# Stick-breaking attention in a hybrid layer: the mask moved into the score's accumulation, and the suffix product made from two float32r products

## The chip, the core and the metric

The kernel runs on one core of one Trainium2 chip. The metric is the device time in microseconds (us). Three runs of the kernel before took 3732.57, 3734.17 and 3734.45 us, so the median is 3734.17 us.

## The reference, cut to what matters

One decoder layer: input projection, stick-breaking attention (8 heads of 64), an S5 state-space part, an output mix and a gated convolutional FFN. It handles a prompt of 2048 tokens, and 8 sample tokens that each attend to 8192 cached keys. The part that changes is this:

```python
z = q @ k.T * HEAD_DIM**-0.5 + bias
mask = k_pos[None, :] < q_pos[:, None]
log_keep = jnp.where(mask, log_sigmoid(-z), 0.0)       # = -softplus(z)
later = cumsum(log_keep, reverse=True) - log_keep      # sum over the keys between s and t
w = jnp.where(mask, exp(log_sigmoid(z) + later), 0.0)
out = w @ v
```

Written with sp = softplus(z), the log of a weight is z minus the sum of sp over this key and all later ones.

## The kernel before, in words

`stage_attention` is one of several stages. Five engines each run a list of their own, with semaphores between them. A *unit* is one block of scores, transposed: 128 keys (index j) by up to 512 queries (chunk c of 4). Per head there are NU = 40 units, chunk 3 first (16 units), then chunk 2 (12), chunk 1 (8) and chunk 0 (4), and in a chunk the keys go from late to early. The first four units of a chunk lie on the diagonal and have 128, 256, 384 and 512 columns; all others are 512 wide. Of the 40 units, 21 are off the diagonal with j > 0.

Each engine runs a loop over steps s = 0..39 for each head, with the stages of a unit software-pipelined over the steps:

- PE at step s: the scores of unit s (`z`, L1415: two float32r products that carry rounded and rest parts and the bias) into one of NZ = 5 PSUM banks. Then for unit u = s - 3: `negtri` (a triangle of -1) times X[u] (L1425), on the diagonal also `ident` times `fillm` (L1428, adds -1e30 where masked), then `negones` times S[u-1] (L1433), and `logw_ready` goes up. Then, at odd u, weights times V for the last two units (L1448), and at even steps up to 32 four pages of the cached V of the sample sequence (L1382). `negtri`, `negones`, `ident` and V products are plain float32.
- ACT at step s: exp (L1197) and ln(1 + .) (L1199) of unit s into X (NX = 4 buffers), then exp of unit s - 3 into Wt (L1205). At some steps it also rounds parts of q and k of the next head (L1169 to L1175).
- DVE at step s: softplus of unit s - 1 from X and the bank (L1302, X in place). At steps 0 to 31 it then multiplies two cached K pages by the query (L1331) and sums over the head dimension (L1336). This is the attention of one sample sequence, which goes along with each head of the prompt.
- POOL (GpSimd) in `sums_round`: on the diagonal X times `keepm` in place (L1135) and into S (L1142); then S[u] = S[u-1] + X[u] (L1148). S has two buffers, so S[u] waits for `logw_ready` of unit u - 1:

```python
pool.wait_ge(logw_ready, b * NU + u)
...
pool.tensor_tensor(new[:, r:], old[:, r:], x[:, r:], ALU.add).then_inc(s_part, 1)
```

  PE reads S[u-1] with unit u, so S[u] is wanted only one unit later.
- SP queues all loads: K pages into a ring of 8 places, V pages into one of 16, and q, k, v of the next head.

Around steps 32 to 37 the sample sequence is finished: a softplus and scans over its 64 pages, `finish_sequence` (DVE L1261 makes `own`, PE L1390 sums it, DVE L1265 keeps it), PE L1456 and L1457, and `turn_queries`. Heads 1 to 6 are a hardware loop; heads 0 and 7 are written out.

Of the kernel before, what the change touches and what calls it, by code (L numbers as in the profile page):

```python
# [22 lines left out]
P = 128  # L23
# [3 lines left out]
NS = 8  # L27
# [877 lines left out]
def stage_attention(nc, A, keep):  # L905
# [16 lines left out]
    MASKS = [sum(diag(v) for v in range(u + 1)) for u in range(NU)]  # L922
    with ExitStack() as ctx:
# [9 lines left out]
        X = m.sb("X", [P, NX, CH])  # L933
        Wt = m.sb("Wt", [P, NW, CH])
        S = m.sb("S", [P, 2, CH])
        o_sb = m.sb("o_sb", [HD, 2, CH])
        o_odd = m.sb("o_odd", [HD, CH])
        bias_all, bias_left = m.sb("bias_all", [P, H]), m.sb("bias_left", [P, H])
        bias_part, bias_rows = m.sb("bias_part", [P, BP, H], F32R), m.sb("bias_rows", [P, H])
        bias_now = m.sb("bias_now", [P, 1])  # L940
        wide = m.sb("wide", [P, CH])
        negtri, negones = m.sb("negtri", [P, P]), m.sb("negones", [P, P])
        one = m.sb("one", [P, 1])
        keepm, fillm = m.sb("keepm", [P, P]), m.sb("fillm", [P, P])
        Kr = m.sb("Kr", [P, KSLOTS, PP, AW])
        Vr = m.sb("Vr", [P, VSLOTS, PP, AW])
        prod = m.sb("prod", [P, 2, PP * AW])
# [4 lines left out]
        table_in = x_s[0:1].bitcast(I32)  # L952
        R = m.sb("R", [P, H, NPG + 1])
        heads = m.sb("heads", [P, AW])
        own = m.sb("own", [P, AW])
# [12 lines left out]
        z_ready, e_ready, l_ready, sp_ready, sp_masked = (  # L968
            m.sem(n) for n in ("z_ready", "e_ready", "l_ready", "sp_ready", "sp_masked"))
# [14 lines left out]
        Q_AT = K_END + 5  # L984
# [28 lines left out]
        with nc.Block() as block:  # L1013
# [93 lines left out]
            def _(pool):  # L1107
                pool.memset(negtri[:], -1.0).then_inc(consts, 1)
                pool.memset(negones[:], -1.0).then_inc(consts, 1)
                pool.memset(keepm[:], 1.0).then_inc(consts, 1)  # L1110
# [4 lines left out]
                pool.wait_ge(consts, 6)  # L1115
                pool.memset(wide[:], 1.0).then_inc(wide_set, 1)
                pool.wait_ge(wide_set, 1)
                pool.memset(kh1[HD:P, :].bitcast(F32), 1.0).then_inc(wide_set, 1)
                pool.wait_ge(wide_set, 2)
# [4 lines left out]
                sel(out=keepm[:], in_=keepm[:], compare_op=ALU.is_gt, fill=0.0, base=0, pattern=[[1, P]],  # L1124
                    channel_multiplier=-1).then_inc(consts, 1)
                sel(out=fillm[:], in_=fillm[:], compare_op=ALU.is_gt, fill=MASKED, base=0, pattern=[[1, P]],
                    channel_multiplier=-1).then_inc(consts, 1)
                pool.wait_ge(consts, 9)

                def sums_round(b):  # L1130
                    for u in range(NU):
                        o, x = cols(u), X[:, u % NX, :]
                        if diag(u):
                            pool.wait_ge(sp_ready, b * NU + u + 1)
                            pool.tensor_tensor(x[:, o:o + P], x[:, o:o + P], keepm[:], ALU.mult).then_inc(sp_masked, 1)  # L1135
                        if U[u][1] == 0:
                            continue
                        old, new = S[:, (u - 1) % 2, :], S[:, u % 2, :]
                        pool.wait_ge(logw_ready, b * NU + u)
                        if diag(u):  # L1140
                            pool.wait_ge(sp_masked, b * MASKS[-1] + MASKS[u])
                            pool.tensor_tensor(new[:, o:o + P], x[:, o:o + P], keepm[:], ALU.mult).then_inc(s_part, 1)  # L1142
                        else:
                            pool.wait_ge(sp_ready, b * NU + u + 1)
                        if steps(u) == 2 or not diag(u):
                            r = o + P if diag(u) else 0
                            pool.wait_ge(s_part, b * SUMS[-1] + SUMS[u - 1])
                            pool.tensor_tensor(new[:, r:], old[:, r:], x[:, r:], ALU.add).then_inc(s_part, 1)  # L1148
# [5 lines left out]
            def _(act):  # L1154
# [3 lines left out]
                act.activation(bias_part[:, 0, :], bias_all[:], ACT.Copy).then_inc(bias_rounded, 1)  # L1158
                for n in range(1, BP):
                    act.wait_ge(bias_cut, n)  # L1160
                    act.activation(bias_part[:, n, :], bias_left[:], ACT.Copy).then_inc(bias_rounded, 1)

                def split(b, c):
# [8 lines left out]
                    if c == NCH - 1:  # L1172
                        act.wait_ge(wide_set, 2)
                        act.wait_ge(bias_now_ready, b + 1)
# [11 lines left out]
                def round_(b, steps, first, last, rest):  # L1186
                    for s in steps:
# [13 lines left out]
                        if u is not None:  # L1201
# [3 lines left out]
                            act.activation(Wt[:, u % NW, cols(u):], bank[:, u % NZ, cols(u):], ACT.Exp).then_inc(w_ready, 1)  # L1205
                        r, u = behind(b, s, LAG + 2, first, rest)
# [19 lines left out]
                        if s == K_END + 5:  # L1226
# [8 lines left out]
            def _(dve):  # L1235
# [4 lines left out]
                dve.wait_ge(consts, 9)  # L1240
# [49 lines left out]
                def round_(b, steps, first, last, rest):  # L1290
                    for s in steps:
# [17 lines left out]
                        if u is not None and U[u][1] == 0:  # L1309
# [5 lines left out]
                            if alone:  # L1315
                                dve.tensor_copy(o_sb[:, c % 2, 0:alone], o_odd[:, 0:alone]).then_inc(alone_copied, 1)
# [1188 lines left out]
```

## Time and profile before

| | us |
|---|---|
| median of three runs | 3734.17 |
| profiled execution, own time | 3731.39 |
| its span | 3729.7 |
| PE busy | 3346.6 (90%) |
| DVE busy | 2056.5 (55%) |
| ACT busy | 1408.0 (38%) |
| POOL busy | 759.2 (20%) |
| attention stage | about 738 to 1797 of the span |

Times below are from the start of the span. PE is the matmul engine, PEld its weight load. "Busy" of overlapping, pipelined matmuls reaches past the moment when the next can start, so a step's cost is read from start to start. A bracket at the end of a line says how long the engine was idle before it and who ended that.

### The profile page before, as it was taken

The page shows a single profiled execution, that of the slowest core. Times are in us where ns is not written, and L with a number is a line of the kernel's source. Part 1 is how long each engine was busy: PE and PEld are TensorE (multiplying, and loading weights), DVE is VectorE, ACT ScalarE, POOL GpSimd, SP SyncE. Part 2 cuts the span into 40 slices and gives each one's busy share as a digit, 9 for nine tenths or more (in the row PEclk, how much of TensorE's full clock was granted, in tenths as well). Part 3 has the DMA queues.
Part 4 walks back from the last instruction along what each step waited for, and adds up shares of the span by engine and source line. Part 5 has one row for each costly group of instructions (what it writes and reads, how often), then busy time and mean ns, then how long its engine had stood idle before and what let it go on. Part 6 is the DMA issues. An engine that isn't in the chain of part 4 may idle for free. (4 is left out here: it accounts for less than half of the span.)

```text
span 3729.7 us, 49239 instructions
## 1 busy us (share of the span) xinstructions
PE 3346.6 (90%) x14901; PEld 2314.4 (62%) x14901; DVE 2056.5 (55%) x2777; ACT 1408.0 (38%) x2214; POOL 759.2 (20%) x903
## 2 busy tenths in 40 slices
PE   4999864589899999999789979999999999999998
PEld 3888742334444443444368857877787778777777
DVE  5110139799798889889245544534553455345542
ACT  4110101256555655665233344423442344223331
POOL 1000047665444444455001100000000000000000
PEclk7999976799999999999789989999999999999999
DMA  3121252397898888888545443343334333433433
GB/s 124 63 73 45 76 72 26 73 290 247 267 304 259 272 283 278 268 274 293 172 136 149 133 122 97 102 138 100 98 105 137 101 97 106 135 125 113 125 116 113
DMA packets 487646, 569.70 MB, mean 153 GB/s; under 512 B 64808, under 2 KB 308616, under 8 KB 485321
## 3 DMA queue, kind: packets, MB, share of 16 engines
q1 hardware_dynamic: 482950, 549.81, 48.0%
q10 hardware_dynamic: 4328, 17.05, 1.2%
q8 instruction: 87, 1.43, 0.2%
q14 instruction: 105, 0.85, 0.1%
q0 software_dynamic: 176, 0.56, 0.0%
HBM read 506.91 MB, written 59.30 MB: 152 GB/s over the span
## 5 line engine op out<-in xcount | busy, mean ns | idle before, releaser
L2132 PE MATMUL ffn_bank<-ffn_xh,ffn_wh 128*128 128x512 f32 x1408 | 557.5, 396 | 18.7 <-DVE ffn_wl L2346 18.2
L2132 PE MATMUL ffn_bank<-ffn_xl,ffn_wh 128*128 128x512 f32 x1408 | 549.3, 390 | 0.0
L2132 PE MATMUL ffn_bank<-ffn_xh,ffn_wl 128*128 128x512 f32 x1408 | 548.6, 390 | 0.0
L1148 POOL TENSOR_TENSOR att_S<-att_S,att_X 128x512 f32<-128x512 f32 (+3 forms) x256 | 307.3, 1200 | 342.1 <-PE att_bank L1433 320.0
L1331 DVE TENSOR_TENSOR att_prod<-att_Kr,att_q_wide 128x1024 f32<-128x1024 f32 x256 | 334.0, 1305 | 5.4 <-issue 4.3
L1425 PE MATMUL att_bank<-att_X,att_negtri 128*128 128x512 f32 (+3 forms) x640 | 301.9, 554 | 32.3 <-POOL att_X L1135 29.6
L2132 PEld LDWEIGHTS ffn_bank<-ffn_xh,ffn_wh 128*128 128x128 f32 x1408 | 264.9, 188 | 94.8 <-DVE ffn_wl L2346 31.0
L1336 DVE TENSOR_REDUCE att_z_s<-att_prod 128x16 f32<-128x1024 f32 x256 | 314.0, 1226 | 8.8
L2132 PEld LDWEIGHTS ffn_bank<-ffn_xh,ffn_wl 128*128 128x128 f32 x1408 | 264.8, 188 | 56.4
L2132 PEld LDWEIGHTS ffn_bank<-ffn_xl,ffn_wh 128*128 128x128 f32 x1408 | 265.1, 188 | 52.4
L2350 DVE TENSOR_TENSOR ffn_wdl<-ffn_wdf,ffn_wdh 128x1024 fp32r<-128x1024 f32 x88 | 107.5, 1225 | 334.0 <-ACT ffn_wdh L2256 333.9
L1197 ACT ACTIVATE att_X<-att_bank 128x512 f32<-128x512 f32 (+2 forms) x320 | 170.9, 534 | 259.4 <-PE att_bank L1415 224.0
L2383 DVE TENSOR_SCALAR ffn_conv<-ffn_gbuf,ffn_prm 128x512 f32<-128x512 f32 x88 | 48.1, 547 | 386.7 <-issue 202.5
L1433 PE MATMUL att_bank<-att_S,att_negones 128*128 128x512 f32 (+3 forms) x576 | 258.9, 532 | 0.0
L2089 POOL TENSOR_TENSOR ffn_st<-ffn_st,kept_eps 128x1 f32<-128x1 f32 x16 | 4.9, 309 | 1216.1 <-ACT ffn_stage L2330 1119.9
L2346 DVE TENSOR_TENSOR ffn_wl<-ffn_stage,ffn_wh 128x1024 fp32r<-128x1024 f32 x176 | 215.2, 1223 | 30.7 <-ACT ffn_wh L2251 29.7
L1205 ACT ACTIVATE att_Wt<-att_bank 128x512 f32<-128x512 f32 (+2 forms) x320 | 169.7, 530 | 163.7 <-PE att_bank L1433 151.5
L2234 PE MATMUL ffn_bank<-ffn_wdh,ffn_hh 128*128 128x512 f32 x704 | 218.6, 392 | 12.1 <-DVE ffn_wdl L2350 9.9
L2256 ACT ACTIVATE ffn_wdh<-ffn_wdf 128x1024 fp32r<-128x1024 f32 x88 | 93.0, 1061 | 344.6 <-PE ffn_bank L2234 315.0
L2234 PE MATMUL ffn_bank<-ffn_wdh,ffn_hl 128*128 128x512 f32 x704 | 218.4, 392 | 0.0
L2234 PE MATMUL ffn_bank<-ffn_wdl,ffn_hh 128*128 128x512 f32 x704 | 217.8, 391 | 0.0
L2251 ACT ACTIVATE ffn_wh<-ffn_stage 128x1024 fp32r<-128x1024 f32 x176 | 186.0, 1057 | 80.6 <-PE ffn_bank L2132 65.2
(379 smaller groups left out, 6096.3 us busy)
## 6 DMA issues: line engine op xcount, KB each, us to landing
att_Kr<-in_cache_k_dram SPq DMA_DIRECT2D x512, 256.0 KB, 3.7
att_Vr<-in_cache_v_dram SPq DMA_DIRECT2D x512, 256.0 KB, 3.8
ffn_wdf<-in_w_down_dram SPq DMA_DIRECT2D x108, 512.0 KB, 3.6
ffn_stage<-in_w_gate_dram SPq DMA_DIRECT2D x89, 512.0 KB, 3.9
ffn_stage<-in_w_up_dram SPq DMA_DIRECT2D x88, 512.0 KB, 4.5
qku_work<-in_x_prompt_dram SPq DMA_DIRECT2D x16, 512.0 KB
att_qf<-qT_dram SPq DMA_DIRECT2D x64, 128.0 KB, 3.7
att_kf<-kT_dram SPq DMA_DIRECT2D x64, 128.0 KB, 3.7
```

The source lines that it names most:

```text
L1148: pool.tensor_tensor(new[:, r:], old[:, r:], x[:, r:], ALU.add).then_inc(s_part, 1)
L1197: act.activation(x, bank[:, s % NZ, cols(s):], ACT.Exp).then_inc(e_ready, 1)
L1205: act.activation(Wt[:, u % NW, cols(u):], bank[:, u % NZ, cols(u):], ACT.Exp).then_inc(w_ready, 1)
L1331: tt(pr, Kr[:, kk % KSLOTS], q_wide[:, None, :].to_broadcast([P, PP, AW]), ALU.mult).then_inc(k_used, 1)
L1336: dve.tensor_reduce(z_s[:, :, kk * PP:(kk + 1) * PP].rearrange("p h r -> p r h"), prod[:, kk % 2, :].rearrange("p (k h d) -> p k h d", k=P ...
L1425: last = pe.matmul(bank[:, u % NZ, o:], negtri[:], X[:, u % NX, o:], start=False, stop=True, skip_group_check=True)
L1433: last = pe.matmul(bank[:, u % NZ, o2:], negones[:], S[:, (u - 1) % 2, o2:], start=False, stop=True, skip_group_check=True)
L2132: mm = pe.matmul(bank[:, first + f % 2, :], w[:, j, k, :], x[:, k, :], start=(k == 0 and n == 0), stop=(k == KD - 1 and n == 2))
L2234: mm = pe.matmul(bank[:, 2 * t + c, :], x[:, f, cols], w[:, sl, c * CH:(c + 1) * CH], start=(f == 0 and n == 0), stop=(f == FT - 1 and n = ...
L2251: act.activation(wh[:, j], wf[:, j], ACT.Copy).then_inc(w_hi[j], 1)
L2346: tt(wl[:, j], wf[:, j], wh[:, j].bitcast(F32), ALU.subtract).then_inc(w_lo[j], 1)
L2350: tt(wdl[:, f % 2, :], wdf[:, f % 2, :], wdh[:, f % 2, :].bitcast(F32), ALU.subtract).then_inc(wd_lo, 1)
```

## The change

On the diagonal the mask `fillm` is now added while the score is built, so exp, ln and softplus see -1e30 and come out as zero, and the multiplications by `keepm` go. The softplus X is split into a rounded part Xh (float32r, by ACT) and a rest Xl = X - Xh (by POOL), and `negtri` times X becomes two float32r products. PE waits for `x_hi` before the first, and for `x_lo` before the second. To make room, `prod` is gone (the K page is multiplied in its ring place), and small tiles share memory. `keep_sequence`, PE's `finish_sequence`, the sums of the sample sequence and what follows them move one step later.

```diff
@@ POOL, sums_round
                     for u in range(NU):
                         o, x = cols(u), X[:, u % NX, :]
-                        if diag(u):
+                        if U[u][1] > 0:
+                            old, new = S[:, (u - 1) % 2, :], S[:, u % 2, :]
+                            pool.wait_ge(logw_ready, b * NU + u)
                             pool.wait_ge(sp_ready, b * NU + u + 1)
-                            pool.tensor_tensor(x[:, o:o + P], x[:, o:o + P], keepm[:], ALU.mult).then_inc(sp_masked, 1)
-                        if U[u][1] == 0:
-                            continue
...
+                            if diag(u):
+                                pool.tensor_tensor(new[:, o:o + P], x[:, o:o + P], one[:].to_broadcast([P, P]), ALU.mult).then_inc(s_part, 1)
+                            if steps(u) == 2 or not diag(u):
+                                r = o + P if diag(u) else 0
+                                pool.wait_ge(s_part, b * SUMS[-1] + SUMS[u - 1])
+                                pool.tensor_tensor(new[:, r:], old[:, r:], x[:, r:], ALU.add).then_inc(s_part, 1)
+                        pool.wait_ge(x_hi, b * NU + u + 1)
+                        pool.tensor_tensor(Xl[:, u % NX, o:], x[:, o:], Xh[:, u % NX, o:].bitcast(F32), ALU.subtract).then_inc(x_lo, 1)
@@ ACT, after Exp into Wt
+                        r, u = behind(b, s, 1, first, rest)
+                        if u is not None and (s == 0 or not rest):
+                            act.wait_ge(sp_ready, r * NU + u + 1)
+                            if not first or u >= NX:
+                                act.wait_ge(logw_ready, units_to(r, u, NX, first))
+                            act.activation(Xh[:, u % NX, cols(u):], X[:, u % NX, cols(u):], ACT.Copy).then_inc(x_hi, 1)
@@ DVE, K pages
-                            pr = prod[:, kk % 2, :].rearrange("p (k c) -> p k c", k=PP)
-                            tt(pr, Kr[:, kk % KSLOTS], q_wide[:, None, :].to_broadcast([P, PP, AW]), ALU.mult
+                            pr = Kr[:, kk % KSLOTS]
+                            tt(pr, pr, q_wide[:, None, :].to_broadcast([P, PP, AW]), ALU.mult
                                ).then_inc(k_used, 1)
@@ PE
                             for q, (key, part) in enumerate(((khl, qhh), (kh1, qlb))):
                                 mm = pe.matmul(bank[:, s % NZ, o:], key[:, j * P:(j + 1) * P], part[:, c * CH + o:(c + 1) * CH],
                                                start=(q == 0), stop=(q == 1))
+                                if q == 0 and diag(s):
+                                    pe.matmul(bank[:, s % NZ, o:o + P], ident[:], fillm[:], start=False, stop=False,
+                                              skip_group_check=True)
...
-                            if diag(u):
-                                pe.wait_ge(sp_masked, r * MASKS[-1] + MASKS[u])
-                            pe.wait_ge(sp_ready, r * NU + u + 1)
-                            last = pe.matmul(bank[:, u % NZ, o:], negtri[:], X[:, u % NX, o:], start=False, stop=True,
+                            pe.wait_ge(x_hi, r * NU + u + 1)
+                            pe.matmul(bank[:, u % NZ, o:], negtri_r[:], Xh[:, u % NX, o:], start=False, stop=True, skip_group_check=True)
+                            pe.wait_ge(x_lo, r * NU + u + 1)
+                            last = pe.matmul(bank[:, u % NZ, o:], negtri_r[:], Xl[:, u % NX, o:], start=False, stop=True,
                                              skip_group_check=True)
-                            if diag(u):
-                                last = pe.matmul(bank[:, u % NZ, o:o + P], ident[:], fillm[:], start=False, stop=True,
-                                                 skip_group_check=True)
```

## Rows read from the trace of the kernel before

**Rows 1.** Windows: busy of PE, PEld, DVE, ACT, POOL; clock, DMA share, GB/s.

```profile
738.00:1797.00 1059.00, 981.39 (x3805) 428.17 (x3809) 913.15 (x1059) 618.33 (x1148) 508.83 (x504) 0.96 0.84 270
1060.00:1100.00 40.00, 40.00 (x168) 16.45 (x170) 39.55 (x42) 22.51 (x42) 21.52 (x22) 1.00 0.97 304
```

**Rows 2.** Timeline of PE: steady step of chunk 3 (unit 11 and neighbours).

```profile
1072.94 0.50 PE L1415 MATMUL att_bank<-att_qhh,att_khl 128*128 128x512 f32 x1
1073.28 0.40 PE L1415 MATMUL att_bank<-att_qlb,att_kh 128*128 128x512 f32 x1
1073.52 1.02 PE L1425 MATMUL att_bank<-att_X,att_negtri 128*128 128x512 f32 x2
1074.37 1.02 PE L1433 MATMUL att_bank<-att_S,att_negones 128*128 128x512 f32 x2
1075.33 1.07 PE L1382 MATMUL att_bank<-att_Vr,att_w_s 128*8 128x512 f32 x8
1076.32 0.50 PE L1415 MATMUL att_bank<-att_qhh,att_khl 128*128 128x512 f32 x1
```

**Rows 3.** Timeline of ACT, DVE and POOL in the same step.

```profile
1073.79 0.60 ACT L1197 ACTIVATE att_X<-att_bank 128x512 f32<-128x512 f32 x1 [1.15 <-PE att_bank L1415]
...
1073.94 1.22 DVE L1331 TENSOR_TENSOR att_prod<-att_Kr,att_q_wide 128x1024 f32<-128x1024 f32 x1
...
1074.42 0.63 ACT L1199 ACTIVATE att_X<-att_X 128x512 f32<-128x512 f32 x1
...
1075.19 1.23 DVE L1336 TENSOR_REDUCE att_z_s<-att_prod 128x16 f32<-128x1024 f32 x1
...
1075.63 1.28 POOL L1148 TENSOR_TENSOR att_S<-att_S,att_X 128x512 f32<-128x512 f32 x1 [2.10 <-PE att_bank L1433]
```

**Rows 4.** Groups of the attention stage, shapes apart: POOL.

```profile
L1148 POOL TENSOR_TENSOR att_S<-att_S,att_X 128x512 f32<-128x512 f32 x168 | 243.7, 1450 | 342.1 <-PE att_bank L1433 320.0 <-DVE att_X L1302 22.1
L1135 POOL TENSOR_TENSOR att_X<-att_X,att_keepm 128x128 f32<-128x128 f32 x128 | 141.0, 1102 | 139.7 <-DVE att_X L1302 137.3 <-PE att_bank L1428 2.4
...
L1148 POOL TENSOR_TENSOR att_S<-att_S,att_X 128x128 f32<-128x128 f32 x32 | 14.7, 458 | 0.0
```

**Rows 5.** Timeline: a POOL operation that meets DVE's L1331, and PE behind it.

```profile
803.95 1.22 DVE L1331 TENSOR_TENSOR att_prod<-att_Kr,att_q_wide 128x1024 f32<-128x1024 f32 x1
804.11 1.37 POOL L1135 TENSOR_TENSOR att_X<-att_X,att_keepm 128x128 f32<-128x128 f32 x1 [0.53 <-DVE att_X L1302]
...
805.54 0.91 PE L1425 MATMUL att_bank<-att_X,att_negtri 128*128 128x384 f32 x2 [1.24 <-POOL att_X L1135]
```

**Rows 6.** Timeline of PE: scores of steps 31, 0, 3, 31, 0 (heads 2, 3).

```profile
1096.02 0.50 PE L1415 MATMUL att_bank<-att_qhh,att_khl 128*128 128x512 f32 x1
...
1128.75 0.33 PE L1415 MATMUL att_bank<-att_qhh,att_khl 128*128 128x128 f32 x1
...
1139.77 0.50 PE L1415 MATMUL att_bank<-att_qhh,att_khl 128*128 128x512 f32 x1
...
1229.36 0.50 PE L1415 MATMUL att_bank<-att_qhh,att_khl 128*128 128x512 f32 x1
...
1262.03 0.33 PE L1415 MATMUL att_bank<-att_qhh,att_khl 128*128 128x128 f32 x1
```

**Rows 7.** Timeline of PE, head 0: scores of steps 4 and 31.

```profile
751.99 0.77 PE L1415 MATMUL att_bank<-att_qhh,att_khl 128*128 128x512 f32 x1
...
833.24 0.80 PE L1415 MATMUL att_bank<-att_qhh,att_khl 128*128 128x512 f32 x1
```

**Rows 8.** Timeline of PE: the sample sequence's finish in step 33.

```profile
1107.09 1.86 PE L1390 MATMUL att_bank<-att_one,att_own 128*128 128x1 f32 x8 [3.81 <-DVE att_own L1261]
```

**Rows 9.** Windows, columns as in rows 1: short gaps of PE, and after a long one.

```profile
804.00:807.00 3.00, 1.76 (x8) 0.90 (x6) 2.96 (x5) 2.07 (x4) 2.52 (x3) 1.00 0.96 316
807.00:810.00 3.00, 2.24 (x9) 0.98 (x9) 2.96 (x5) 1.73 (x3) 2.83 (x3) 1.00 0.88 307
1107.00:1112.00 5.00, 4.91 (x15) 3.69 (x16) 2.96 (x12) 1.23 (x2) 0.00 (x0) 0.50 0.97 317
```

More of the change, by code:

```diff
@@ L921, in stage_attention @@
     SUMS = [sum(steps(v) for v in range(u + 1)) for u in range(NU)]
-    MASKS = [sum(diag(v) for v in range(u + 1)) for u in range(NU)]
     with ExitStack() as ctx:
@@ L933, in stage_attention @@
         X = m.sb("X", [P, NX, CH])
+        Xh, Xl = m.sb("Xh", [P, NX, CH], F32R), m.sb("Xl", [P, NX, CH], F32R)
         Wt = m.sb("Wt", [P, NW, CH])
         S = m.sb("S", [P, 2, CH])
-        o_sb = m.sb("o_sb", [HD, 2, CH])
+        o_all = m.sb("o_all", [P, CH])
+        o_sb = [o_all[k * HD:(k + 1) * HD, :] for k in range(2)]
         o_odd = m.sb("o_odd", [HD, CH])
-        bias_all, bias_left = m.sb("bias_all", [P, H]), m.sb("bias_left", [P, H])
+        bias_all = m.sb("bias_all", [P, H])
         bias_part, bias_rows = m.sb("bias_part", [P, BP, H], F32R), m.sb("bias_rows", [P, H])
         bias_now = m.sb("bias_now", [P, 1])
-        wide = m.sb("wide", [P, CH])
         negtri, negones = m.sb("negtri", [P, P]), m.sb("negones", [P, P])
+        negtri_r = m.sb("negtri_r", [P, P], F32R)
         one = m.sb("one", [P, 1])
-        keepm, fillm = m.sb("keepm", [P, P]), m.sb("fillm", [P, P])
+        fillm = m.sb("fillm", [P, P])
         Kr = m.sb("Kr", [P, KSLOTS, PP, AW])
         Vr = m.sb("Vr", [P, VSLOTS, PP, AW])
-        prod = m.sb("prod", [P, 2, PP * AW])
         qsT = m.sb("qsT", [P, QT, NS + 1])
@@ L1158, in _ @@
                 act.activation(bias_part[:, 0, :], bias_all[:], ACT.Copy).then_inc(bias_rounded, 1)
+                act.wait_ge(consts, 7)
+                act.activation(negtri_r[:], negtri[:], ACT.Copy).then_inc(tri_ready, 1)
                 for n in range(1, BP):
                     act.wait_ge(bias_cut, n)
-                    act.activation(bias_part[:, n, :], bias_left[:], ACT.Copy).then_inc(bias_rounded, 1)
+                    act.activation(bias_part[:, n, :], bias_left, ACT.Copy).then_inc(bias_rounded, 1)
                 def split(b, c):
@@ L1172, in split @@
                     if c == NCH - 1:
-                        act.wait_ge(wide_set, 2)
+                        if isinstance(b, int) and b == 0:
+                            act.wait_ge(wide_set, 1)
                         act.wait_ge(bias_now_ready, b + 1)
@@ L1270, in spread_queries @@
                     dve.wait_ge(q_turned, b)
+                    if not (isinstance(b, int) and b < 2):
+                        dve.wait_ge(col_ready, b - 1)
                     dve.tensor_copy(qrep[:], qsT[:, :, bass.ds(b, 1)].to_broadcast([P, QT, P])).then_inc(q_spread, 1)
@@ L1340, in round_ @@
                             finish_sequence(b - 1)
-                        if s == K_END + 2 and not first:
+                        if s == K_END + 3 and not first:
                             keep_sequence(b - 1)
@@ L1460, in round_ @@
                             samples_v(b - 1, s - 1)
-                        if s == K_END + 1 and not first:
+                        if s == K_END + 2 and not first:
                             finish_sequence(b - 1)
```

59 lines of the change are left out of this document (24 added, 35 removed).

## The prediction

> **What bounds the kernel now.** I read the page first, then the windows, to find the stage that changes. Attention takes 1059 us of the span, with PE busy 981, DVE 913, ACT 618 and POOL 509 [rows 1]. In the thick of a head PE is busy all of the time, DVE 39.55 of 40 us, and the DMA engines have a share of 0.97 [rows 1]. So I went to the timeline, to see what a step costs and who is behind whom. A full step takes 1076.32 - 1072.94 = 3.38 us on PE with no gap: scores 0.58, `negtri` 0.85, `negones` 0.96, cached V 0.99 [rows 2]. POOL needs 1.28 for its sum and then waits for PE's `logw_ready` (2.10 us idle before it) [rows 3]. PE sets the step, and POOL has slack.
>
> **What is removed from PE.** `negtri` times a full X costs 0.85. A float32r product of the same width costs 0.24 from start to start (1073.28 to 1073.52), or 0.34 when it is the first after a wait (1072.94 to 1073.28) [rows 2]. Two cost 0.48, so 0.37 is saved in a full step, which leaves PE 3.01 of work. A head's units have 17408 columns, as much as 34 full ones: 12.6 us a head, 101 us over eight, if PE's work were all. The mask product `fillm` only moves to the score.
>
> **What is removed from POOL.** The 128 in-place `keepm` products (1.10 us mean [rows 4]). They stood before PE on the diagonal.
>
> **What is added to ACT.** One copy per unit, about 0.63 at full width like the ln beside it [rows 3]. The step becomes 2.5 us, under any step length below, and Xh is made two units before PE wants it: I cost it at nothing. If ACT had no slack, it would be 0.63 a step.
>
> **What is added to POOL, and where it lies.** This is the step that decides. Xl of unit u is a subtraction with two SBUF inputs. No row has its output type, so I take the sum's own 1.28 [rows 3]; bounds are 1.28 and the 1.45 that the sum averages with its blocked cases [rows 4]. POOL does Xl[u] behind S[u], and S[u] waits for `logw_ready` of unit u-1. PE does `negones` of unit u, and so `logw_ready` of u, behind the wait for Xl[u]. Before, S[u] had a whole unit of time; now unit u cannot end until POOL has done two full operations after the end of unit u-1. Walk the ring:
>
> - start of `negones` to the start of POOL's sum: 1075.63 - 1074.37 = 1.26 [rows 2, 3]
> - sum 1.24 to the next start (durations overlap by some 0.04), then Xl 1.28
> - POOL's end to PE's start: 804.11 + 1.37 to 805.54 = 0.06 [rows 5]
> - PE's Xl product after a wait, to the start of `negones`: 0.34
>
> That is 4.18 us, against 3.38. PE fills 3.01 of it and waits.
>
> **DVE's part.** POOL's 128-column product took 1.37 us where 0.46 is usual [rows 4, 5]: it started 0.16 after DVE's L1331 and ended 0.31 after L1331 did. So a POOL operation stands still while L1331 runs, and then takes its own time less some 0.15. In the new ring, counted from `negones`, the next score starts at 1.95, exp at 2.80, ln ends at 4.06, softplus takes 0.6, and L1331 runs from 4.7 to 5.92. POOL's next sum would start at 4.18 + 1.26 = 5.44, in the middle of it, and ends at 5.92 + 0.31 + 0.82 (the full 1.28 less 0.46 of the short one) = 7.05. The rest of the ring (1.24 + 0.06 + 0.34 = 1.64) puts the `negones` two ahead at 8.69, that is T + T, so T = 4.35. Xl then runs well before L1331 (done at about 4.0, against 4.7).
>
> Trainium skill, "SBUF — State Buffer", section "Who interferes with whom": a DVE instruction with two SBUF inputs and a GpSimd one that reads SBUF exclude each other, and the one that starts first keeps the ports for its whole length. Rows 5 agree. By it L1331 could also take the ports between sum and Xl; that is the second rival.
>
> **The sum for a head.** From the score of step 3 to that of step 31 are units 0 to 27: before, 1229.36 - 1139.77 = 89.6 us [rows 6]. After: 18 heavy units (off the diagonal, j > 0) at 4.35 = 78.3; two with j = 0, which have no S, at PE's 3.0 = 6.0; eight on the diagonal. For these the ring has shorter operations (0.46 at 128 columns, 1.28 at 512 [rows 3, 4], 0.73 and 1.01 between) and I get 2.0 to 2.5, 2.75 (DVE's own work), 3.25 and 4.1 with POOL unblocked, and take 2.5, 2.9, 3.7 and 4.5, twice 13.6 = 27.2. Sum 111.5, so +21.9. Steps 31 to 39: 1128.75 - 1096.02 = 32.7 before [rows 6]. Ring: 2.5 + 2.9 + 3.1 + 4.1, three heavy at 4.2 (no L1331 here), 2.5 and 2.2 = 29.9, and 2 for the sample sequence's products = 32. Here PE now loses 3.81 us to `own` and then runs at half clock (0.50 [rows 8, 9]); the move by a step and an idle DVE take that away, and the ring spends it: -0.7. Steps 0 to 2: 11.0 before, +1 for POOL's way round the loop. A head gains +22.2, seven are +155. Head 0 has no cached V and runs faster now (751.99 to 833.24 for steps 4 to 30 [rows 7], about 83 with step 3), and the ring is no faster there: 111.5 - 83 + 1 = +29. Together +184.
>
> Setup constants, DVE's in-place K product (same shape, same release of the ring) and the longer waits for q: nothing, as they lie beside the projection's end or repeat what was there. DMA gets easier, since the steps are longer.
>
> 3731.39 (profiled execution, span 3729.7) + 184 = 3915; the median of the runs stands 2.8 above it: 3918.
>
> Bounds. Low: T = 4.07 (no restart cost, no blocking), diagonal 12.3, and the end of the head 4 shorter: +10 a head, +20 for head 0, 3824. High: T = 4.6 (both operations at 1.45, little overlap), diagonal 15.5, the end 3 longer and the start 2: +36 a head, +38, 4024.
>
> **Rivals.**
>
> 1. *PE's saving counts (ends faster).* For it: PE is the busiest, and POOL's spans are rough. Against: the waits of PE and ACT line up with POOL's ends. It decides where sum and Xl together take under 3.38 - 1.26 - 0.06 - 0.34 = 1.72 us; the rows give 2.5. Then -101, with the gap at `own` up to -140: 3633, or 3594.
> 2. *L1331 gets in between sum and Xl.* The sum ends, L1331 is waiting, and Xl stands for 1.22: T = 5.4 in the 18 heavy units of the K steps, diagonal 15.5 a chunk. Against: L1331 follows ln, and lies after Xl by 0.7. 97 + 6 + 31 = 134, +44 a head, +51: 3734 + 359 = 4093.
> 3. *The clock falls.* PE would idle 1.3 us in each 4.35. Rows 9: with gaps of 1.24 and 0.76 us and 4.0 of 6 us busy, the clock stayed at 1.00 (2.4 GHz), and it went to 0.50 (1.2 GHz) after the 3.81 gap. At 0.50 PE's own 3.01 is about 5.7 a step, no gap is left, and the clock would return; for half of the steps, T = 5.0 and short units 0.7 longer: +43 a head, 4080 in all.
> 4. *No change.* The ring, but the diagonal and the end of the head give back 16 to 20 us a head. Only some 8 at `own` are in sight (3.81, and about 4 at half clock). 3734.
>
> The Trainium skill, "TensorE: Matmul & The Clock Gate", section "A second HAM failure mode: psum-queue depth-cycling", tells of a kernel in which small idle times between groups of matmuls made the clock go to and fro. The trace shows it not for gaps of this length, only over a few steps.
>
> **How the numbers follow.** Forecast 0.76, rival 1 0.04, rival 2 0.09, rival 3 0.09, rival 4 0.02. The forecast's own range is 3824 to 4024; rivals 2 and 3 lie just above, so I reach up to 4090, which leaves out rival 1, rival 4, part of rivals 2 and 3 and the forecast's edges. Within 0.2% is what a measurement of this kernel can't tell from no change. Faster 0.04, same 0.02, slower 0.94.
>
> **What would show it.** Right: in K steps of chunk 3 PE's scores stand 4.2 to 4.5 us apart; PE's second `negtri` product waits over 1 us, with POOL's Xl as what ends it; POOL has two full operations on end, then waits for `logw_ready`; PE busy in the stage falls though the stage grows to some 1240 us; the clock stays 1.00. Wrong: score starts 3.0 apart (rival 1), 5.4 apart with L1331 between sum and Xl (rival 2), float32r products of 0.43 and more (rival 3), or POOL's Xl far from 1.28.

## The result, and the profile after

The changed kernel takes 3971.76 us (median of 4 runs, 3969.16 to 3973.63). The kernel before took 3733.37 beside it. The ratio is 1.0643, with a 95% interval of 1.0625 to 1.0662: slower by 238 us, where 184 were forecast. The time lies in the range (3824 to 4090).

The page of the changed kernel, its span and its part 1:

```profile
span 3971.8 us, 49820 instructions
...
PE 3366.6 (85%) x14901; PEld 2311.9 (58%) x14901; DVE 2111.4 (53%) x2777; ACT 1553.4 (39%) x2535; POOL 1026.7 (26%) x1092
```

The span is 242.1 longer. First, where? These are windows of the changed kernel: the attention stage, steps 3 to 30 of head 3, two stretches of head 0, then a spell in head 3 and what follows it.

```profile
738.00:2040.00 1302.00, 996.94 (x3797) 423.68 (x3800) 967.92 (x1060) 767.30 (x1472) 777.66 (x696) 0.92 0.69 220
745.00:816.00 71.00, 43.65 (x105) 19.11 (x103) 54.59 (x54) 36.15 (x68) 37.31 (x30) 0.72 0.73 215
816.00:868.00 52.00, 36.42 (x106) 16.30 (x102) 38.20 (x38) 25.55 (x50) 31.64 (x27) 0.79 0.74 236
1239.92:1357.10 117.18, 89.13 (x352) 34.99 (x348) 97.66 (x97) 65.78 (x122) 73.00 (x62) 0.96 0.88 276
1252.00:1262.00 10.00, 8.24 (x26) 3.53 (x26) 9.90 (x10) 5.15 (x10) 6.50 (x6) 0.79 0.73 225
1262.00:1285.00 23.00, 16.03 (x63) 5.46 (x62) 20.23 (x20) 12.08 (x21) 14.72 (x11) 1.00 0.78 243
```

The stage takes 1302 us, against 1059 [rows 1], so all of the time is in it. PE and DVE no longer fill it. Which heads? The start of a head's first score, on PE's timeline of the changed kernel, for heads 0, 1 and 7:

```profile
742.41 0.48 PE L1422 MATMUL att_bank<-att_qhh,att_khl 128*128 128x128 f32 x1 [4.23 <-DVE att_khl L1289]
...
911.36 0.33 PE L1422 MATMUL att_bank<-att_qhh,att_khl 128*128 128x128 f32 x1
...
1870.67 0.33 PE L1422 MATMUL att_bank<-att_qhh,att_khl 128*128 128x128 f32 x1
```

Before, these stood at 738.56, 864.21 and 1661.37. So head 0 went from 125.7 to 169.0 us (+43.3), and heads 1 to 6 from an average of (1661.37 - 864.21) / 6 = 132.9 to (1870.67 - 911.36) / 6 = 159.9 (+27.0 each). With the later start (+3.9) that makes 209; nearly all that is left falls in head 7 (about +28).

Where in a head? The same timeline around head 3: its step 0, 3 and 31, and step 0 of head 4, to be laid beside [rows 6].

```profile
1230.45 0.33 PE L1422 MATMUL att_bank<-att_qhh,att_khl 128*128 128x128 f32 x1
...
1239.92 0.50 PE L1422 MATMUL att_bank<-att_qhh,att_khl 128*128 128x512 f32 x1
...
1357.16 0.50 PE L1422 MATMUL att_bank<-att_qhh,att_khl 128*128 128x512 f32 x1
...
1389.72 0.33 PE L1422 MATMUL att_bank<-att_qhh,att_khl 128*128 128x128 f32 x1
```

| us, head 3 | before [rows 6] | after | change | forecast |
|---|---|---|---|---|
| steps 0 to 2 | 11.0 | 9.5 | -1.5 | +1 |
| steps 3 to 30 | 89.6 | 117.2 | +27.6 | +21.9 |
| steps 31 to 39 | 32.7 | 32.6 | -0.1 | -0.7 |

Other heads from 1 to 6 show 7.9 to 9.5, 117.2 to 121.6 and 31.8 to 32.8. The loss is in the steps with K pages. Two of them on PE, changed kernel ([rows 2] show one of before):

```profile
1262.33 0.40 PE L1433 MATMUL att_bank<-att_Xh,att_negtri_r 128*128 128x512 f32 x1
1264.60 0.50 PE L1435 MATMUL att_bank<-att_Xl,att_negtri_r 128*128 128x512 f32 x1 [1.87 <-POOL att_Xl L1142]
1264.94 1.02 PE L1440 MATMUL att_bank<-att_S,att_negones 128*128 128x512 f32 x2
...
1266.88 0.50 PE L1422 MATMUL att_bank<-att_qhh,att_khl 128*128 128x512 f32 x1
...
1268.84 0.51 PE L1435 MATMUL att_bank<-att_Xl,att_negtri_r 128*128 128x512 f32 x1 [1.00 <-POOL att_Xl L1142]
1269.18 1.02 PE L1440 MATMUL att_bank<-att_S,att_negones 128*128 128x512 f32 x2
```

POOL in the same steps:

```profile
1261.05 1.28 POOL L1140 TENSOR_TENSOR att_S<-att_S,att_X 128x512 f32<-128x512 f32 x1 [2.06 <-PE att_bank L1440]
1262.29 2.26 POOL L1142 TENSOR_TENSOR att_Xl<-att_X,att_Xh 128x512 fp32r<-128x512 f32 x1
1266.20 1.36 POOL L1140 TENSOR_TENSOR att_S<-att_S,att_X 128x512 f32<-128x512 f32 x1 [1.65 <-PE att_bank L1440]
1267.52 1.27 POOL L1142 TENSOR_TENSOR att_Xl<-att_X,att_Xh 128x512 fp32r<-128x512 f32 x1
```

And DVE:

```profile
1261.84 1.58 DVE L1337 TENSOR_TENSOR att_Kr<-att_Kr,att_q_wide 128x1024 f32<-128x1024 f32 x1
1263.45 1.22 DVE L1342 TENSOR_REDUCE att_z_s<-att_Kr 128x16 f32<-128x1024 f32 x1
...
1265.18 1.23 DVE L1337 TENSOR_TENSOR att_Kr<-att_Kr,att_q_wide 128x1024 f32<-128x1024 f32 x1
```

Read the three together. PE waits for POOL's Xl, POOL waits for PE's `negones`, and between them POOL does sum and Xl: that is the forecast's ring. But Xl takes 2.26 us once and 1.27 the next time. The K product (L1337, before: L1331) started while the sum ran and ended at 1263.42, 1.09 after the sum did; Xl, started at 1262.29, ended at 1264.55, 1.13 after the K product did. So each stood until the other was through. Two `negones` lie 5.14 us apart (1259.80 to 1264.94), the next two 4.24. The waits of the stage, changed kernel (us in total, times, longest):

```profile
PEld att_bank L1435 <- POOL att_Xl L1142: 387.3, 275, 3.5
POOL att_S L1140 <- PE att_bank L1440: 291.4, 159, 3.7
PE att_bank L1435 <- POOL att_Xl L1142: 283.7, 235, 3.1
```

POOL's full-width groups of the stage, by form:

```profile
L1142 POOL TENSOR_TENSOR att_Xl<-att_X,att_Xh 128x512 fp32r<-128x512 f32 x224 | 328.4, 1470 | 5.8 <-ACT att_Xh L1208 5.8
L1140 POOL TENSOR_TENSOR att_S<-att_S,att_X 128x512 f32<-128x512 f32 x168 | 230.1, 1370 | 305.8 <-PE att_bank L1440 291.4 <-DVE att_X L1308 14.3
```

### The profile page after: what moved, and what is told of

Read it like the earlier page. It is cut to its first block and busy times, and to the rows that moved or that the text cites. A ratio compares the mean times of both kernels' runs of the same rounds, so it can differ in the third digit from the quotient of the medians.

```text
span 3971.8 us, 49820 instructions
## 1 busy us (share of the span) xinstructions
PE 3366.6 (85%) x14901; PEld 2311.9 (58%) x14901; DVE 2111.4 (53%) x2777; ACT 1553.4 (39%) x2535; POOL 1026.7 (26%) x1092
## 5 line engine op out<-in xcount | busy, mean ns | idle before, releaser
L1142 POOL TENSOR_TENSOR att_Xl<-att_X,att_Xh 128x512 fp32r<-128x512 f32 (+2 forms) x320 | 413.9, 1297 | 5.8 <-ACT att_Xh L1208 5.8
L1435 PE MATMUL att_bank<-att_Xl,att_negtri_r 128*128 128x512 f32 (+2 forms) x320 | 155.0, 484 | 285.1 <-POOL att_Xl L1142 283.7
L1140 POOL TENSOR_TENSOR att_S<-att_S,att_X 128x512 f32<-128x512 f32 (+3 forms) x256 | 293.3, 1146 | 305.8 <-PE att_bank L1440 291.4
L1337 DVE TENSOR_TENSOR att_Kr<-att_Kr,att_q_wide 128x1024 f32<-128x1024 f32 x256 | 360.7, 1409 | 4.7 <-issue 4.2
L1342 DVE TENSOR_REDUCE att_z_s<-att_Kr 128x16 f32<-128x1024 f32 x256 | 313.2, 1223 | 8.8
L1435 PEld LDWEIGHTS att_bank<-att_Xl,att_negtri_r 128*128 128x128 f32 x320 | 63.7, 199 | 389.2 <-POOL att_Xl L1142 387.3
L1308 DVE SCALAR_TENSOR_TENSOR att_X<-att_X,att_bank 128x512 f32<-128x512 f32 (+2 forms) x320 | 192.7, 604 | 167.3 <-ACT att_X L1196 166.3
L1440 PE MATMUL att_bank<-att_S,att_negones 128*128 128x512 f32 (+3 forms) x576 | 280.1, 571 | 0.0
L1194 ACT ACTIVATE att_X<-att_bank 128x512 f32<-128x512 f32 (+2 forms) x320 | 170.4, 532 | 149.5 <-PE att_bank L1422 127.3
L2263 ACT ACTIVATE ffn_wdh<-ffn_wdf 128x1024 fp32r<-128x1024 f32 x88 | 92.8, 1059 | 341.4 <-PE ffn_bank L2241 313.9
```

The source lines that it names most:

```text
L1142: pool.tensor_tensor(Xl[:, u % NX, o:], x[:, o:], Xh[:, u % NX, o:].bitcast(F32), ALU.subtract).then_inc(x_lo, 1)
L1194: act.activation(x, bank[:, s % NZ, cols(s):], ACT.Exp).then_inc(e_ready, 1)
L1308: stt(x, x, LN_TOP, z, ALU.min, ALU.max).then_inc(sp_ready, 1)
L1337: tt(pr, pr, q_wide[:, None, :].to_broadcast([P, PP, AW]), ALU.mult).then_inc(k_used, 1)
L1342: dve.tensor_reduce(z_s[:, :, kk * PP:(kk + 1) * PP].rearrange("p h r -> p r h"), pr.rearrange("p k (h d) -> p k h d", h=H), AX.X, ALU.add ...
L1435: last = pe.matmul(bank[:, u % NZ, o:], negtri_r[:], Xl[:, u % NX, o:], start=False, stop=True, skip_group_check=True)
```

## The experiments

Each kernel was timed in three rounds beside the kernel before (3732.31 us beside the first four, 3732.82 beside the next four, 3734.28 beside the last four). "Steps 3 to 30" are those of head 3, from score to score.

| kernel | us | ratio to before, 95% | steps 3 to 30, us |
|---|---|---|---|
| before | 3733.37 | | 89.6 |
| after | 3971.76 | 1.0643 (1.0625 to 1.0662) | 117.2 |
| e1_xl_first | 3800.44 | 1.0177 (1.0159 to 1.0196) | 100.1 |
| e6_s_early | 3797.34 | 1.0168 (1.0151 to 1.0185) | 100.5 |
| e3_after_no_kmul | 3864.3 | 1.0353 (1.0334 to 1.0371) | 106.7 |
| e4_xl_free | 3718.01 | 0.9956 (0.9942 to 0.9971) | 90.2 |
| e2_mask_only | 3705.52 | 0.9923 (0.9905 to 0.9941) | 89.7 |
| e7_after_lag2 | 3964.85 | 1.0625 (1.0606 to 1.0644) | 114.1 |
| e8_xl_first_lag2 | 3779.53 | 1.0133 (1.0116 to 1.015) | 94.9 |
| e9_xl_free_lag2 | 3705.18 | 0.992 (0.9898 to 0.9943) | 86.1 |
| e10_half_split | 3742.88 | 1.0027 (1.0016 to 1.0039) | 91.5 |
| e12_late_split | 3708.24 | 0.9929 (0.9912 to 0.9946) | 89.2 |
| e11_xl_first_lag2_no_kmul | 3702.12 | 0.9911 (0.9894 to 0.9927) | 86.9 |
| e13_mask_only_no_kmul | 3685.33 | 0.9864 (0.9847 to 0.988) | 87.5 |

### Is it the ring? Break it in two places

**e1_xl_first**: POOL does Xl before the sum, so Xl no longer stands behind PE's `logw_ready`.

```diff
+                        pool.wait_ge(x_hi, b * NU + u + 1)
+                        pool.tensor_tensor(Xl[:, u % NX, o:], x[:, o:], Xh[...], ALU.subtract).then_inc(x_lo, 1)
                         if U[u][1] > 0:
                             pool.wait_ge(logw_ready, b * NU + u)
...
-                        pool.wait_ge(x_hi, b * NU + u + 1)
-                        pool.tensor_tensor(Xl[:, u % NX, o:], ...)
```

> The changed kernel with POOL's two operations of a unit in the other order: Xl[u] first, then S[u]. The same work on every engine. Ring theory (the time is lost because PE's logw_ready of unit u waits for S[u] and Xl[u] of the same unit): Xl no longer stands behind the wait for unit u-1, so the ring of 4.2 to 4.35 us goes. What is left in steps with a K product is the time for which sum, Xl and L1337 exclude each other, 1.28 + 1.28 + 1.22 = 3.78 us, so such steps come down from 4.35 to 5.2 to about 3.7 and the kernel to about 3820 us, still above before. Load theory (POOL simply has too much to do, in whatever order): no change, about 3970 us.

**e6_s_early**: POOL's order stays; PE does `negones` before the Xl product and frees S with a semaphore of its own.

```diff
-                            pool.wait_ge(logw_ready, b * NU + u)
+                            pool.wait_ge(s_read, b * READS[-1] + (READS[u - 1] if u else 0))
@@ PE: Xh product, then
+                                pe.matmul(bank[...], negones[:], S[:, (u - 1) % 2, o2:], ...).then_inc(s_read, 1)
+                            pe.wait_ge(x_lo, r * NU + u + 1)
+                            pe.matmul(bank[...], negtri_r[:], Xl[:, u % NX, o:], ...).then_inc(logw_ready, 1)
```

> The ring broken at another place: POOL's order stays sum, then Xl, but PE does negones ahead of the Xl product and tells POOL right after it that S has been read, so that the next sum needs neither Xl nor the end of the unit. Ring theory: the gain of putting Xl first comes back, full steps at 3.5 us (what sum, Xl and L1337 leave, 3.48 measured), 3790 to 3810 us. If putting Xl first helped because Xh is used sooner or L1337 falls better, and not by the ring: 3850 us or more.

Both give back over 170 us (3971.76 to 3800.44 and 3797.34), with all of the change's work still there. The ring is the main cause. Neither gets to the time before: the scores of their K steps (steps with a K product) are 3.44 to 3.53 us apart. POOL's timeline in e1_xl_first shows what limits them:

```profile
1190.65 2.00 POOL L1132 TENSOR_TENSOR att_Xl<-att_X,att_Xh 128x512 fp32r<-128x512 f32 x1 [0.22 <-ACT att_Xh L1208]
1192.62 1.27 POOL L1142 TENSOR_TENSOR att_S<-att_S,att_X 128x512 f32<-128x512 f32 x1
1194.11 2.04 POOL L1132 TENSOR_TENSOR att_Xl<-att_X,att_Xh 128x512 fp32r<-128x512 f32 x1 [0.21 <-ACT att_Xh L1208]
```

DVE in the same steps:

```profile
1189.83 1.69 DVE L1337 TENSOR_TENSOR att_Kr<-att_Kr,att_q_wide 128x1024 f32<-128x1024 f32 x1
...
1193.28 1.72 DVE L1337 TENSOR_TENSOR att_Kr<-att_Kr,att_q_wide 128x1024 f32<-128x1024 f32 x1
```

POOL is idle 0.2 of each 3.46 us, though its two operations are 2.5 us of work: in each of these steps the K product waits for the sum (1.7 instead of 1.22) and Xl for the K product (2.0 instead of 1.27).

### The K product alone

**e3_after_no_kmul**: the changed kernel, with the K product on one column.

```diff
-                            tt(pr, pr, q_wide[:, None, :].to_broadcast([P, PP, AW]), ALU.mult
-                               ).then_inc(k_used, 1)
+                            tt(pr[:, 0, 0:1], pr[:, 0, 0:1], q_wide[:, 0:1], ALU.mult).then_inc(k_used, 1)
```

> The changed kernel with DVE's K product L1337 cut to one column, which leaves out the products of the sample sequence's scores. Ring with port exclusion: nothing gets between sum and Xl, heavy steps are all 4.18 us and evenly spaced, 18 x 4.18 + 6 + 25 = 106 us for steps 3 to 30 where the changed kernel takes 119.6, and the total about 3865 us. If the alternation of 4.2 and 5.2 us comes from the clock or from ACT: it stays, and the total is within 20 us of 3972.

3864.3, so the K product costs the changed kernel 107 us. What is left is the bare ring. PE's timeline of e3_after_no_kmul:

```profile
1215.94 1.02 PE L1439 MATMUL att_bank<-att_S,att_negones 128*128 128x512 f32 x2
...
1217.90 0.50 PE L1421 MATMUL att_bank<-att_qhh,att_khl 128*128 128x512 f32 x1
...
1219.77 0.50 PE L1434 MATMUL att_bank<-att_Xl,att_negtri_r 128*128 128x512 f32 x1 [0.91 <-POOL att_Xl L1142]
1220.11 1.02 PE L1439 MATMUL att_bank<-att_S,att_negones 128*128 128x512 f32 x2
```

POOL, between those two `negones`:

```profile
1217.20 1.29 POOL L1140 TENSOR_TENSOR att_S<-att_S,att_X 128x512 f32<-128x512 f32 x1 [1.65 <-PE att_bank L1439]
1218.45 1.27 POOL L1142 TENSOR_TENSOR att_Xl<-att_X,att_Xh 128x512 fp32r<-128x512 f32 x1
```

The terms: 1217.20 - 1215.94 = 1.26, 1.25 to Xl's start, 1.27, 0.05 to PE, 0.34: 4.17, where the prediction worked out 4.18. Windows of the same kernel, steps 3 to 30 of head 3:

```profile
1191.30:1298.00 106.70, 84.17 (x352) 32.93 (x349) 64.45 (x97) 65.13 (x123) 62.13 (x62) 1.00 0.93 297
```

The clock stays at 1.00 with PE idle for 0.91 us in each 4.15.

### What is behind the ring: is PE's saving there to be had?

**e4_xl_free** drops Xl; PE multiplies Xh twice instead, so PE's work and ACT's copy stay and POOL's addition goes. **e2_mask_only** keeps the mask half of the change (and the moved steps of the head's end) and takes the split out: no Xh, no Xl, one float32 `negtri` product.

```diff
@@ e4_xl_free
-                        pool.tensor_tensor(Xl[:, u % NX, o:], ...).then_inc(x_lo, 1)
...
-                            pe.wait_ge(x_lo, r * NU + u + 1)
-                            last = pe.matmul(bank[...], negtri_r[:], Xl[:, u % NX, o:], ...
+                            last = pe.matmul(bank[...], negtri_r[:], Xh[:, u % NX, o:], ...
@@ e2_mask_only: besides Xl, no copy into Xh, and
+                            pe.wait_ge(sp_ready, r * NU + u + 1)
+                            last = pe.matmul(bank[...], negtri[:], X[:, u % NX, o:], ...
```

> The changed kernel without POOL's subtraction and without PE's wait for it: PE multiplies Xh a second time in place of Xl, so the rest of the softplus is left out of the sum and PE's work stays that of the changed kernel. It is the most that PE's saving could give. Ring theory: full steps at PE's 3.0 to 3.1 us, 12 us a head under before and more for the end of the head, 3600 to 3640 us. If ACT's copy or DVE or the DMA engines bound the steps by themselves (DVE's work is 3.0 us a step, DMA share 0.97 before): 3.2 to 3.4 us a step and 3680 to 3730 us.

> Half of the change alone: the mask in the score's accumulation, no keepm products, the later places of the sample sequence's steps, but negtri times X as one float32 product, with no Xh and no Xl. If only the split costs: full steps are back at 3.38 us, the diagonal is free of POOL's blocked products and PE's wait for own is gone, 3 to 8 us a head less than before: 3675 to 3710 us. If the in-place K product, the shared tiles or the moved steps cost something of their own: 3733 us or above.

e2_mask_only is 27 us faster than before: the good half. Its steps 3 to 30 take what they took (89.7), but steps 31 to 39 take 27 to 30 us in five of heads 1 to 6 instead of 32.7, and the wait before `own` is 1.60 where it was 3.81 [rows 8] (head 2; the tile is now called `att_qrep`). e4_xl_free is slower than that, although its K steps off the diagonal are 2.96 to 3.00 apart. It loses the gain again in two steps of 6.98 and 5.97 (heads 2 to 4), one just behind the diagonal of chunk 3, one behind that of chunk 2. PE's timeline of e4_xl_free in the first:

```profile
1157.85 0.50 PE L1431 MATMUL att_bank<-att_Xh,att_negtri_r 128*128 128x512 f32 x1 [2.07 <-ACT att_Xh L1206]
```

And ACT's:

```profile
1157.17 0.63 ACT L1206 ACTIVATE att_Xh<-att_X 128x512 fp32r<-128x512 f32 x1 [2.17 <-DVE att_X L1306]
1157.38 0.49 ACTq L1218 DMA_DIRECT2D attT_dram<-att_o_all  x1
1158.11 0.60 ACT L1192 ACTIVATE att_X<-att_bank 128x512 f32<-128x512 f32 x1 [0.32 <-issue]
```

ACT stands before its Xh copy until DVE's softplus is done, and the exp of the next unit stands behind it. PE's products behind that wait run at half clock as well (granted 0.50 from 1158.4 to 1161.5). So I moved the copy a unit later, ahead of the exp into Wt, in three kernels:

```diff
+                        r, u = behind(b, s, 2, first, rest)
+                        if u is not None and (s < 2 or not rest):
+                            act.wait_ge(sp_ready, r * NU + u + 1)
...
+                            act.activation(Xh[:, u % NX, cols(u):], X[:, u % NX, cols(u):], ACT.Copy).then_inc(x_hi, 1)
                         r, u = behind(b, s, LAG, first, rest)
...
-                        r, u = behind(b, s, 1, first, rest)
```

> The changed kernel with ACT's copy Xh taken one step later (unit s-2 at step s, ahead of the exp into Wt). Same work. Coupling theory: at the end of a chunk ACT stands at Xh[s-1] until DVE's softplus of that unit, and DVE stands in front of that softplus until ACT's o_odd, which costs one stall of 2 to 3 us and a spell at half clock in chunks 3 and 2. With the copy one step later it goes: 4 to 6 us a head less, 3925 to 3940 us, while the ring's 4.2 to 5.2 us stay. Rival (those long steps are POOL's ring and the clock alone): unchanged, 3972 us.

> Both repairs: Xl[u] ahead of S[u] on POOL, and ACT's copy one step later. Against the kernel with Xl first alone (3800 us): full steps stay at 3.48 us, which is the time for which sum, Xl and L1337 exclude each other, and the two long steps of a head (6.13 and 5.80 us) fall to about 3.5: 5 to 6 us a head less, about 3755 us. So still above before (3732), as 3.48 is above 3.38. If the long steps have another cause: 3800 us.

> The kernel without the subtraction (PE multiplies Xh twice, the rest of the softplus is left out) with ACT's copy one step later. Coupling theory: its full steps are at 2.98 us already, and only the two long steps of a head (6.98 and 5.97 us) and the half clock after them keep it at 3718: 7 to 9 us a head less, 3645 to 3665 us, which is PE's saving at last. If DVE or the DMA engines hold it at that level: 3700 us or more, and steps over 3.1 us.

e7 gains 7 us only: this wait is no large part of the changed kernel's loss, and the theory that it was is down. With the ring broken it is worth 21 (e8), without Xl 13 (e9). e8's long steps are gone, but its steps 0 to 2 take 10.6 us instead of 8.2, and it ends 25 above what I expected. e9 was the strongest test of PE's saving. It misses the 3645 to 3665 of the theory by 40 and comes out level with e2_mask_only. Windows, steps 3 to 30 of head 3, e9_xl_free_lag2:

```profile
1135.59:1221.70 86.11, 80.19 (x353) 33.12 (x349) 84.62 (x90) 62.48 (x118) 50.54 (x32) 1.00 0.93 299
```

DVE is busy for 84.62 of 86.11 us: once PE is relieved, DVE has next to no room, 3.5 us a head below the time before (4.5 to 4.9 in heads 2, 4 and 6). Whether DVE alone sets that level is not shown, as e11 below reaches no lower without the K product. So part of PE's saving is there: steps 3 to 30 take 694 us over the eight heads, in e2 724. The ends of the heads give it back. Steps 31 to 39 take 32.9 to 34.5 us in heads 2 to 6, in e2 27.0 to 30.0. PE waits there for ACT's copy, twice in head 3, for 1.53 and 2.70 us, and the clock over its steps 31 to 39 is 0.85, in e2 1.00. The second wait (PE, e9_xl_free_lag2):

```profile
1233.22 0.50 PE L1431 MATMUL att_bank<-att_Xh,att_negtri_r 128*128 128x512 f32 x1 [2.70 <-ACT att_Xh L1200]
```

### Splitting only some units

**e10_half_split** splits the even units (Xl first, copy a unit later), **e12_late_split** only units 31 to 39, where there are no K pages. Both set `cut2` and fall back to `negtri` times X elsewhere:

```diff
+    cut2 = lambda u: u % 2 == 0        # e12_late_split: u >= 31
...
+                            if cut2(u):
...
+                            else:
+                                pe.wait_ge(sp_ready, r * NU + u + 1)
+                                last = pe.matmul(bank[...], negtri[:], X[:, u % NX, o:], ...
```

> Mask in the accumulation, Xl first, copy one step later, and the split for units with even u only; odd u multiply by negtri in plain float32 as before. Per two full steps PE has 3.01 + 3.38 = 6.39 us, the ports 2 x 1.22 + 2 x 1.28 + 1.28 = 6.3 less some overlap: 3.2 us a step, 0.18 less than with the mask alone (3705 us), over some 28 steps a head: 3665 to 3695 us. If POOL's three operations in two steps meet L1337 badly: 3.4 us a step and 3705 us or more.

> The mask alone for units 0 to 30, the split (Xl first, copy one step later) for units 31 to 39 only, which PE takes up in steps that have no K product. Five of them are full: at most 5 x 0.37 and some for the narrow ones, 2 us a head, if PE is what those steps wait for: 3685 to 3700 us against 3705 for the mask alone. If they wait for DVE and ACT (PE's clock is 0.85 to 0.90 there, it stands idle often): 3700 to 3715 us, no difference.

e10 missed by 48 us and more. Windows of its steps 3 to 30, head 3:

```profile
1146.20:1237.70 91.50, 87.05 (x352) 33.98 (x348) 90.38 (x90) 55.65 (x104) 53.02 (x46) 0.98 0.93 296
```

DVE is busy for 90.38 of 91.50 us, 5.8 more than in e9 with the same 90 instructions. Standing for POOL counts as busy, and DVE has no time to spare here. e12 can't be told from e2_mask_only: where there are no K pages, the split gains nothing either.

### Without DVE's K product, is the saving real?

Both kernels leave out the K product as e3 does.

> The split with Xl first and the copy one step later, and DVE's K product cut to one column (leaves out the products of the sample sequence's scores), so that neither DVE nor the shared ports bind. Theory (the saving is hidden by DVE's 84 to 86 us for steps 3 to 30 and by the ports): full steps at PE's 3.0 us, 77 to 82 us for steps 3 to 30, total 3630 to 3670 us. If POOL's own 2.5 us a step or the DMA engines (1.05 MB a full step) bind instead: 3.2 to 3.4 us a step, 86 to 90 us.

> The mask alone with the K product cut to one column in the same way: the partner of the split kernel without it. PE holds full steps at 3.38 us with or without DVE, so steps 3 to 30 stay at 88 to 90 us and the total at 3690 to 3705 us. Theory: the split's saving then shows as the difference of the two, 0.37 us a full step and 30 to 60 us in all. Rival: the split saves nothing even so, both alike.

Another miss for me: e11 was to take 3630 to 3670 us, and the split kernel is 17 us slower than the mask alone, even without the K product. Most of that is not in the steady steps. Head 0 alone takes 124.2 us against 114.5, head 4 131.5 against 127.3, while steps 3 to 30 of heads 1 to 6 are 0.4 to 1.7 us a head shorter in e11. Windows of steps 3 to 30, head 3, first e11_xl_first_lag2_no_kmul:

```profile
1133.64:1220.50 86.86, 83.42 (x352) 33.91 (x348) 69.09 (x88) 61.30 (x118) 61.74 (x60) 0.98 0.93 296
```

then e13_mask_only_no_kmul:

```profile
1121.94:1209.40 87.46, 87.46 (x352) 34.66 (x348) 63.29 (x89) 49.70 (x90) 31.36 (x32) 1.00 0.92 297
```

In e13 PE is full. In e11 it has 3.4 us free, and no other engine is near it. The DMA engines carry 296 and 297 GB/s in the two; the other kernels with steps 3 to 30 of 86 to 92 us show 293 to 302. Waits of e11, 1100 to 1600:

```profile
POOL att_Xl L1132 <- ACT att_Xh L1202: 177.0, 139, 4.0
...
DVE att_Kr L1337 <- DMA att_Kr<-in_cache_k_dram: 33.0, 25, 2.6
```

DVE now waits for K pages. That would make the stream of cached pages the next limit, but the traces don't single it out. The same wait is longer in e13, where PE is full:

```profile
DVE att_Kr L1329 <- DMA att_Kr<-in_cache_k_dram: 54.7, 32, 3.4
```

e3 shows the same 297 GB/s in steps that take 106.7 us, and e9 passes below 87 us with 0.93 and 299 GB/s. No kernel took the load away, so what holds e11 stays open.

## Why the prediction was right, and what was off

**The ring: right, in place and size.** 4.17 against 4.18 us (e3), and breaking it in POOL's order or in PE's gives back 171 and 174 us. Of the signs named beforehand, two stand in the trace: POOL's two full operations on end before its wait for `logw_ready`, and PE's second product waiting 1.0 to 1.9 us for Xl. Two stand in part: scores 4.2 to 4.4 us apart in some steps and 5.1 to 5.2 in others, and a stage that grew, but to 1302 us and not 1240. Two don't: PE's busy time in the stage did not fall (981 before [rows 1], 997 after; products at the lower clock last longer, and e3's window at a clock of 1.00 has 84.17 where the changed kernel's has 89.13), and the clock did not stay at 1.00.

**The K product on the port (T = 4.35): the term that was mis-sized.** The forecast let it cost 0.17 us in 18 steps of 8 heads, 24 us. e3 measures 107. Removing the same work gives 77 where the ring is broken (e8 to e11), and 20 where there is no split (e2 to e13); so some 87 of the 107 come with the split, where the forecast had 24. I had placed L1331 behind its step's ln, after Xl, "done at about 4.0, against 4.7". In the second half of chunk 3 that holds: scores at 1119.64, 1124.04, 1128.35 and 1132.72 in head 2, 4.3 to 4.4 apart. But on the diagonal DVE falls behind, and then it works off its backlog at a pace of its own: K products at 1261.84, 1265.18, 1268.17, 1271.64, 3.0 to 3.5 us apart, in a ring of over 4. So their place in the ring slides, and until DVE has caught up, in every other step one lies between sum and Xl. That is rival 2's mechanism, at half its rate: 5.1 to 5.2 us, then 4.25. I treated the phase of DVE as locked to PE; in this trace it is locked only when DVE has caught up.

Trainium skill, "SBUF — State Buffer", section "Who interferes with whom": the one of the two that starts first keeps the ports for its whole length. By that rule either order can occur, and the trace agrees: the K product's 1.58 and Xl's 2.26 us stand one behind the other.

**The clock (rival 3): in part.** I expected 1.00. Steps 3 to 30 of head 3 have 0.96. The clock is 0.50 from 1249.5 to 1252.8 and again from 1256.4 to 1259.6, and the steps there take 5.67 and 6.03 us. The first spell begins as PE ends a wait of 2.02 us for an Xl, the second follows one of 1.76:

```profile
1249.45 0.69 PE L1435 MATMUL att_bank<-att_Xl,att_negtri_r 128*128 128x384 f32 x1 [2.02 <-POOL att_Xl L1142]
1249.94 1.05 PE L1440 MATMUL att_bank<-att_S,att_negones 128*128 128x256 f32 x2
```

(PE, changed kernel.) The length of the last wait doesn't settle it. In e3 the same `negones` pair follows a wait of 1.03 in head 3 and in head 2, and takes 0.59 in the one and 1.05, at half clock, in the other. What the spells cost by themselves was not measured. The stage has a granted clock of 0.92, in e3 0.95, before 0.96 [rows 1], so part of their price is inside the 107 us.

**Head 0: wrong base, and a larger loss.** I took about 83 us for steps 3 to 30; from score to score they took 93.0, since step 3 is held up before the first row that I used. The rise is +39.9 (to 132.9) in place of the forecast's 28.5. There PE has no cached V, and the clock is 0.72 and 0.79 against 0.88 and 1.00 before. e3 has 116.3 there, so 16.6 of it is again the K product and what it brings.

**Steps 0 to 2: sign wrong in heads 2 to 6, small.** +1 was forecast. Heads 0 and 1 show +1.3 and +1.2, heads 2 to 6 -1.5 to -2.9, head 7 +0.4: 16 us under the forecast in all. **Steps 31 to 39: right**, -0.7 against 0.0 to -1.4 in heads 1 to 6 (+2.1 in head 0); the wait before `own` fell from 3.81 to 0.72 and the ring took the gain. Rival 4 needed the diagonal and the end of a head to give back 16 to 20 us; the end gave 1.4 at most.

**The sum of it.** The span grew by 242 where 184 were forecast. Steps 3 to 30 of the eight heads grew by 244 in place of 182. Of these 62, the K product has 78 (it lengthens these steps by 102, as e3 shows, and the forecast held 24.5), the rest of the ring took 6 less than forecast, and head 0's base was 10 too low, which made its rise too large. Steps 0 to 2 gave back 16. Steps 31 to 39, what follows them in head 7, and the later start cost 12 more than forecast. So the ring was right by its working, but that 3918 lies only 54 from 3972 is in part luck: errors of some 32 us the other way hid as much of the K product's.

**Xl at 1.28: right.** 1.27 alone, 1.47 on average with its standing. **ACT's copy at nothing: nearly right in this kernel.** Placed a unit later it gives 7 us; its place is worth 13 to 21 once POOL's ring or Xl is gone, and in e9 PE still waits for it at the end of a head.

**Rival 1 is false even without the ring.** The forecast's 101 us of PE's work don't reach the total: with Xl free (e9) the kernel gets to 3705, where the mask alone stands without any split. Some 30 show in steps 3 to 30, and the ends of the heads give them back. DVE, at 39.55 of 40 us [rows 1], was about as full as PE from the start.

**Open.** What holds e11's steps 3 to 30 at 86.9 us, and why its head 0 is slow; why the later copy lengthens steps 0 to 2; the clock's own share. The best kernel that computes all of the reference is the mask half alone (3705.5, 0.9923), and e12 is level with it; e9, without the rest Xl, is no faster.

## What to carry to other kernels

Before a product is split to relieve the busiest engine, count who makes the new operands and behind which release they stand: here two operations came to lie between one unit's end and the next one's, on an engine that was busy for only 509 of 1059 us. The same look shows whether a second engine is as full as the first; if so, expect little from relief of one until the other is relieved too. And when two engines share a port, don't fix their phase on paper: price both orders, and the alternation of the two.

## What the runs showed of the hardware

- Exclusion goes both ways in turn. In the K steps of e1_xl_first off the diagonal a DVE product stands 0.5 us for POOL's sum and POOL's next operation 0.75 us for the product. It shows only as longer durations, not as a wait.
- A POOL subtraction with float32r output takes the same 1.27 us at 128x512 as a float32 sum.
- PE idle for 0.9 of each 4.15 us left the granted clock at 1.00 over 107 us (e3, head 3). On the diagonal a wait of 2.02 us came with a fall to 0.50 (changed kernel), and so did one of 1.03 in head 2 of e3, while one of the same 1.03 in its head 3 did not.
